# mLSTM iterations of a hybrid decoder layer: scores first, transposes of h in the second block, VectorE scales h late, ScalarE evacuates the transposes

## What is computed

```python
Dm = jnp.exp(jnp.where(causal, logD, -jnp.inf))
S = jnp.einsum('bhtd,bhsd->bhts', qc, kc) * Dm
num = jnp.einsum('bhts,bhsv->bhtv', S, vc) + g[..., None] * jnp.einsum('bhtd,bhdv->bhtv', qc, C)
den = jnp.sum(S, axis=-1) + g * jnp.einsum('bhtd,bhd->bht', qc, n)
h = num / jnp.maximum(jnp.abs(den), jnp.exp(-m_t))[..., None]
C_new = decay[..., None, None] * C + jnp.einsum('bhs,bhsd,bhsv->bhdv', w, kc, vc)
...
h = _rms(h, g_mh).astype(x.dtype).reshape(B, T, M_WIDTH)
m_out = jax.nn.sigmoid(om) * h * jax.nn.silu(zm)
```

## Time and profile before

| | |
|---|---|
| median of 3 runs | 566.33 us (566.26 to 566.77) |
| the profiled execution's own time | 566.57 us |
| its span, first to last instruction | 564.8 us |
| TensorE busy | 552.8 us (98%) |
| VectorE busy | 309.3 us (55%) |
| ScalarE busy | 225.0 us (40%) |
| GpSimd busy | 139.6 us (25%) |
| mean granted TensorE clock | 0.996 of full speed |

### The profile page before, as it was taken

The page is one execution under the profiler, slowest core; times in us unless marked ns, Lnnn a source line. Parts: engine busy times, 40 slices in busy tenths (PEclk is TensorE's granted clock), DMA queues, the critical chain, the costliest instruction groups (busy, mean ns, idle before and its releaser), DMA issues.

```text
span 564.8 us, 10012 instructions
## 1 busy us (share of the span) xinstructions
PE 552.8 (98%) x3999; PEld 511.7 (91%) x3999; DVE 309.3 (55%) x598; ACT 225.0 (40%) x591; POOL 139.6 (25%) x140
## 2 busy tenths in 40 slices
PE   7999999999999999999999999999999999999994
PEld 7999999999999999999989888899999998888773
DVE  5720002492656565521377777534676667778837
ACT  6852221423354434521355454233413126545422
POOL 1001122112334233332011211135533531001203
PEclk9999999999999999999999999999999999999998
DMA  8752210823111011007014231454121003203425
GB/s 312 294 201 76 66 38 3 252 89 85 38 39 38 3 38 39 9 32 182 9 38 141 63 79 57 114 209 165 39 75 37 1 1 111 75 1 118 161 77 204
DMA packets 31606, 50.98 MB, mean 90 GB/s; under 512 B 4460, under 2 KB 23148, under 8 KB 30904
## 3 DMA queue, kind: packets, MB, share of 16 engines
q1 hardware_dynamic: 31128, 49.82, 27.6%
q10 hardware_dynamic: 432, 0.53, 0.3%
HBM read 42.74 MB, written 8.05 MB: 90 GB/s over the span
## 4 chain that ended last, share of the span: by engine, by line
PE 92%; DVE 3%; DMA 1%; issue 1%; ACT 1%; POOL 1%; DVEq 0%; SPq 0%; ACTq 0%
PE ps L627 52%; PE ps L887 4%; PE ps L886 4%; PE ps L885 4%; PE ps L565 3%; PE ps L566 3%; PE ps L567 3%; PE ps L679 2%; PE ps L739 2%; PE ps L804 1%; PE ps L570 1%; PE ps L569 1%; PE ps L780 1%; PE ps L816 1%; PE ps L702 1%
## 5 line engine op out<-in xcount | busy, mean ns | idle before, releaser
L627 PE MATMUL ps<-x_hl,w_hi 128*128 128x364 f32 (+1 forms) x1200 | 303.0, 332 | 1.8 <-DVE x_hl L1277 1.0
L627 PEld LDWEIGHTS ps<-x_hl,w_hi 128*128 128x128 f32 x1200 | 211.1, 188 | 9.7 <-issue 6.5
L627 PE MATMUL ps<-x_hl,w_lo 128*128 128x364 f32 (+1 forms) x600 | 197.9, 330 | 0.0
L627 PEld LDWEIGHTS ps<-x_hl,w_lo 128*128 128x128 f32 x600 | 112.8, 188 | 0.1
L1847 POOL TENSOR_TENSOR qmT<-qmT,sg 128x364 f32<-128x364 f32 (+1 forms) x24 | 35.1, 1465 | 48.8 <-DVE sg L1661 29.0
L1045 ACT ACTIVATE prob<-prob,nmx 128x192 f32<-128x192 f32 (+1 forms) x64 | 27.9, 437 | 45.9 <-DVE sd L1425 45.9
L1799 POOL TENSOR_TENSOR prob<-prob,rden 128x768 f32<-128x768 f32 (+1 forms) x16 | 22.6, 1413 | 72.2 <-DVE rden L1431 72.2
L565 PE MATMUL ps<-wt_hi,x_hl 128*128 128x324 f32 x128 | 39.9, 311 | 0.0
L567 PE MATMUL ps<-wt_hi,x_hl 128*128 128x324 f32 x128 | 39.8, 311 | 0.0
L566 PE MATMUL ps<-wt_lo,x_hl 128*128 128x324 f32 x128 | 39.8, 311 | 0.0
L365 POOL TENSOR_TENSOR w_lo<-w_raw,w_hi 128x1024 fp32r<-128x1024 f32 x12 | 28.7, 2395 | 42.6 <-ACT w_hi L968 42.6
(11 more groups left out here) (286 smaller groups left out, 946.5 us busy)
## 6 DMA issues: line engine op xcount, KB each, us to landing
w_raw<-in_w_in_tiles SPq DMA_DIRECT2D x24, 512.0 KB, 3.6
x_tok<-in_x_prompt SPq DMA_DIRECT2D x8, 512.0 KB, 5.7
x_res<-in_x_prompt SPq DMA_DIRECT2D x8, 512.0 KB, 4.7
wt_raw<-in_w_tok SPq DMA_DIRECT2D x4, 648.0 KB, 8.0
logw<-lw_rows SPq DMA_DIRECT2D x8, 256.0 KB, 4.4
Cs<-in_state_C SPq DMA_DIRECT2D x16, 128.0 KB, 2.5
out_C_sample<-Cs SPq DMA_DIRECT2D x16, 128.0 KB, 1.9
wq_a<-in_w_out_blocks SPq DMA_DIRECT2D x2, 1024.0 KB, 6.6
```

Source lines behind the costliest of these rows:

```text
L627: last = mm(ps[:, sub_bank(sub), 0:w], wt, xm, start=(at_ == 0), stop=(at_ == 23))
```

## The change

It does these things, all in the mLSTM stage:

- TensorE's iteration becomes: scores of unit it, numerator and state update of unit it-1, 12 projection matmuls, transposes of h of unit it-2, `sample_inter` and `sample_round` of round it-1, transposes of k, 12 projection matmuls. `numerator(0)` of the samples moves to the start of iteration 10, the last two transposes of h to the middle of iterations 10 and 11.
- `sample_inter` writes into columns 364 on of the projection bank whose sub has just been evacuated, no more into bank 4. So it waits for that sub's evacuation and no longer for `st_done`; `sample_round` no longer waits for `it_evac`, and a sub that reuses such a bank does.
- `h_transposes` waits for `sd_mul` of the same iteration, `m_scores` for `hT_evac` of three units before.
- VectorE: mask first, then evacuation, gate of q, scores times decay, then denominator, state, mean square, low parts of weights, `inter_second`, and only then the scaling of h, which now also waits for `hT_done` of the unit before.
- ScalarE: takes over the evacuation of the transposes (four `ACT.Copy` with `gmh` as scale), writes the squares into buffers of their own (`h_junk`) instead of `hs`, and so no longer waits there for `hT_done`; `d_exp` comes first, `g_exp` one iteration early at the end.

```diff
+    h_junk = [sb(f"h_junk{h}", [P, P], F32, at_) for h, at_ in enumerate((n + 25728, n + 26240, Wr + 9216, Wr + 9728))]
...
-    IT0 = 320
+    IT0 = 364
+
+    def inter_bank(r):
+
+        return sub_bank(S_P3 + r)
...
+                    if S_P3 + 2 <= sub < S_P3 + 2 + N_ROUND:
+                        wait(pe, "it_evac", sub - S_P3 - 1)
...
         def m_scores(u):
...
-            wait(pe, "hT_evac", u - 2)
+            wait(pe, "hT_evac", u - 3)
...
         def sample_inter(r):
...
-            wait(pe, "st_done", r)
+            wait(pe, "proj_free", S_P3 + r + 1)
...
-                last = mm(ps[PQ * c:PQ * (c + 1), 4, IT0:IT0 + W1], qmT[:, h, T_P + PQ * half:T_P + PQ * (half + 1)],
+                last = mm(ps[PQ * c:PQ * (c + 1), inter_bank(r), IT0:IT0 + W1], qmT[:, h, T_P + PQ * half:T_P + PQ * (half + 1)],
...
         def sample_round(r):
             h, q = r // 2, r % 2
             wait(pe, "st_done", r)
-            wait(pe, "it_evac", r + 1)
...
         def h_transposes(u, it):
...
-            wait(pe, "sd_done", min(it, NTILE))
+            wait(pe, "sd_done", min(it + 1, NTILE))
...
         for it in range(S_P4 - S_P3):
-            if 3 <= it <= NC + 1:
-                h_transposes(it - 2, it)
-            if 2 <= it <= NC + 1:
-                numerator(it - 1)
-                state_update(it - 1)
-            project(7)
-            if it == NC + 2:
-                h_transposes(NC, it)
-                numerator(0)
             if it <= NC:
                 m_scores(it)
+            if 2 <= it <= NC + 2:
+                numerator(it - 1 if it <= NC + 1 else 0)
+            if 2 <= it <= NC + 1:
+                state_update(it - 1)
+            project(12)
+            if it >= 3:
+                h_transposes(it - 2 if it <= NC + 2 else 0, it)
             if 1 <= it <= N_ROUND:
                 sample_inter(it - 1)
-            project(7)
-            if it == NC + 3:
-                h_transposes(0, it)
-            if 1 <= it <= N_ROUND:
                 sample_round(it - 1)
             if it <= NC:
                 k_transposes(it)
-            project(10)
+            project(12)
...
         def h_squares(u):
...
             wait(act, "hden_done", v)
-            wait(act, "hT_done", v - 1)
             wait(act, "hq_ready", v - 1)
...
+        def hT_evac(u):
+            _, off, n = unit_tokens(u)
+            v = H_ORDER.index(u) + 1
+            wait(act, "hT_done", v)
+            for h in range(MH):
+                last = A_(qmT[:, h, off:off + n], ps[:, 1, h * n:(h + 1) * n], ACT.Copy, scale=gmh[:, h:h + 1])
+            last.then_inc(s("hT_evac"), 1)
+
+        g_exp(0)
         for it in range(S_P4 - S_P3):
             if it <= NC:
-                g_exp(it)
+                d_exp(it)
             if 2 <= it <= NC + 2:
                 h_squares(it - 1 if it <= NC + 1 else 0)
+            if it >= 3:
+                hT_evac(it - 2 if it <= NC + 2 else 0)
...
-            if it <= NC:
-                d_exp(it)
             if it <= NC:
                 k_weight(it)
+            if it < NC:
+                g_exp(it + 1)
             evac(S_P3 + it)
...
         for it in range(S_P4 - S_P3):
-            evac(S_P3 + it - 1)
-            if it >= 3:
-                hT_evac(it - 2 if it <= NC + 2 else 0)
-            done = None
-            if 2 <= it <= NC + 2:
-                done = it - 1 if it <= NC + 1 else 0
-                h_denominator(done)
             if it <= NC:
                 mask_weights(it)
-            if 2 <= it <= NC + 1:
-                state(it - 1)
-            if 1 <= it <= N_ROUND and it % 2 == 0:
-                inter_second(it - 1)
-            if done is not None:
-                h_mean_square(done)
-                h_scale(done)
+            evac(S_P3 + it - 1)
             if it <= NC:
                 q_gate(it)
                 sd_mul(it)
             if it == 0:
                 sample_extras()
+            done = None
+            if 2 <= it <= NC + 2:
+                done = it - 1 if it <= NC + 1 else 0
+                h_denominator(done)
+            if 2 <= it <= NC + 1:
+                state(it - 1)
+            if done is not None:
+                h_mean_square(done)
             if it >= 1:
                 splits(S_P3 + it - 1)
+            if 1 <= it <= N_ROUND and it % 2 == 0:
+                inter_second(it - 1)
+            if done is not None:
+                h_scale(done)
```

More of the change, by code:

```diff
@@ L1122, in h_squares @@
             wait(act, "hden_done", v)
-            wait(act, "hT_done", v - 1)
             wait(act, "hq_ready", v - 1)
             for h in range(MH):
-                last = A_(hs[0:n, h, :], ps[0:n, 2 + h // 2, (h % 2) * W1:(h % 2) * W1 + MD], ACT.Square,
+                last = A_(h_junk[h][0:n, :], ps[0:n, 2 + h // 2, (h % 2) * W1:(h % 2) * W1 + MD], ACT.Square,
                           accum_out=hss[0:n, h:h + 1])
             last.then_inc(s("sq_done"), 1)
+        def hT_evac(u):
[6 more added lines that the diff above has]
+        g_exp(0)
         for it in range(S_P4 - S_P3):
             if it <= NC:
-                g_exp(it)
+                d_exp(it)
             if 2 <= it <= NC + 2:
                 h_squares(it - 1 if it <= NC + 1 else 0)
+            if it >= 3:
+                hT_evac(it - 2 if it <= NC + 2 else 0)
             if 1 <= it <= N_ROUND and it % 2 == 1:
                 wait(act, "it_done", it)
-                A_(ITs[:, it // 2, :], ps[:, 4, IT0:IT0 + W1], ACT.Copy, scale=inter_msk[:, 0:1]).then_inc(s("it_evac"), 1)
-            if it <= NC:
-                d_exp(it)
+                A_(ITs[:, it // 2, :], ps[:, inter_bank(it - 1), IT0:IT0 + W1], ACT.Copy, scale=inter_msk[:, 0:1]).then_inc(s("it_evac"), 1)
             if it <= NC:
                 k_weight(it)
+            if it < NC:
+                g_exp(it + 1)
             evac(S_P3 + it)
@@ L1522, in inter_second @@
             part = ITs[:, r // 2, :]
-            STT(out=part, in0=ps[:, 4, IT0:IT0 + W1], scalar=inter_msk[:, 1:2], in1=part, op0=ALU.mult, op1=ALU.add)\
+            STT(out=part, in0=ps[:, inter_bank(r), IT0:IT0 + W1], scalar=inter_msk[:, 1:2], in1=part, op0=ALU.mult, op1=ALU.add)\
                 .then_inc(s("it_evac"), 1)
@@ L1551, in h_scale @@
             wait(dve, "hf_ready", v)
+            wait(dve, "hT_done", v - 1)
             TT(hs[0:n, :, :].rearrange("p (b h) v -> p b h v", b=2), num_view(n)[:, :, :, 0:MD],
@@ L1554, in h_scale @@
                 .then_inc(s("h_done"), 1)
[L1556 to L1561, removed]
         def splits(sub):
```

## The result

The changed kernel takes **562.94 us** (median of 4 runs, 562.81 to 563.21) against 566.51 us of the kernel before on the same chip (566.26 to 566.77, 4 runs): a ratio of 0.9935, with a 95% interval of 0.9923 to 0.9947, or 3.57 us less. The forecast was 563.8, the range 562.6 to 565.6.

A forecast was written before the change was run, and what follows sets the result against it. TensorE, busy for 98% of the span, was taken to bound the kernel. Terms of -2.6, -0.9, +0.9 and +0.15 sum to -2.5 us, from 566.33 to 563.8 us, range 562.6 to 565.6.

The forecast's parts named there:

- The stall goes: TensorE at the transposes of h: scores times decay comes earlier on VectorE, transposes later; 2.61 us of stalls go.
- The new wait and what is queued behind it: VectorE: `sd_mul` waits for the numerator, denominator and state follow; 1.85 us left at the transposes, 0.9 at `sample_round`.
- The rival of a new wait at `sample_round`: TensorE loses 0.25 us in two of three iterations, 1.3 us come back; chance 0.12, shared with dear edges.
- Scaling of h: Last on VectorE, after 1.76 us of waiting for GpSimd; 2.2 us left before the next numerator needs it.
- Evacuation on ScalarE: Four evacuations of the transposes of h take 1.14 us on ScalarE, hidden with 2.2 us to spare.
- Edges: TensorE's changes of tile shape: one of three goes per iteration at 0.10 us each, -0.9 us over eight.
- lower end (-2.5, both free): Case for TensorE's shape changes in which both new ones cost nothing: -2.5 us instead of -0.9.
- the sentence of the Trainium skill: Weight loads overlap only into other row groups; fewer shape changes on TensorE would then save nothing, sum 564.7 us.
- The start: Iteration 0 opens with the samples' scores, which wait for the last q sub's evacuation: +0.9 us, once.
- The end of the stage: Iterations 9 to 11: two more transposes of h have a projection matmul behind them, +0.15 us; samples' numerator 0.
- The rival that the gain is lost before the end: After the mLSTM stage, weights loaded after C is stored come too late: 566 us; chance 0.03.
- The distance from scores to scores: Sign on TensorE that the forecast is right: 9.6 to 9.7 us in every one of iterations 3 to 8.

The follow-up runs named there:

- experiment 3: Kernel before, with only VectorE's scaling of h moved behind the gate of q and scores times decay: 563.63 us, ratio 0.9955.
- experiment 4: Changed kernel with VectorE's gate of q and scores times decay moved behind denominator and state: 566.95 us, ratio 1.0013 to the kernel before.
- experiment 5: Changed kernel with evacuation of the transposes of h back on VectorE: 562.76 us, against 562.52 for the changed kernel in the same set.
- experiment 2: Changed kernel with seven of the last 12 projection matmuls put between `sample_inter` and `sample_round`: 564.02 us, ratio 0.9962 to the kernel before.
- Experiment 1: Changed kernel with the samples' scores of iteration 0 behind the first 12 projection matmuls: 561.79 us, ratio 0.9921 to the kernel before.
- experiment 6: Kernel before with VectorE's gate and scores times decay ahead of scaling h, `sample_inter` directly ahead of `sample_round` and in projection banks: 561.81 us, ratio 0.9925.

## Why the prediction was right, and where its sizes were off

The mechanism and the sign were right, and the time lies inside the range of 562.6 to 565.6, near its lower end. Of the forecast 2.5 us less, 3.6 came. By the parts of the prediction:

1. *The stall goes*, -2.61: right. No idle is booked at L856, and experiment 3 got 2.41 by VectorE's order alone, without the hole that belongs to `sample_inter`. The working took an iteration of 9.79 us as clean, where 9.77 is the average (experiment 3), so the stalls were rather 2.7. Scores times decay starts at N+0.30 (306.98 against 306.68) rather than N+0.20; 1.75 us are left, worked out 1.85.
2. *The new wait and what is queued behind it*: right. State ends at 308.38 + 1.12 = 309.50 = N+2.82, worked out N+2.73, and `sample_round` comes at 310.45 = N+3.77, as worked out. 0.8 us are left, worked out 0.9. The rival of a new wait at `sample_round` didn't come true. A wait of such a size did in experiment 4, at the transposes, where denominator and state are ahead of scores times decay: 4.46 us are lost.
3. *Scaling of h*, end at N+5.5: 321.79 with N = 316.25 is N+5.54. In iterations 4 and 7 it was N+6.45 (313.13 in iteration 4) because of GpSimd's slow operation. The prediction put the low parts of weights into the wait for GpSimd and took that for free. It was not free, but the margin covered it: the numerator came at N+7.78 (314.46), so 1.2 us were left of the 2.2.
4. *Evacuation on ScalarE*, hidden: right in size (1.14 us for four) and in margin (2.1 us), and experiment 5 shows that it brings nothing either.
5. *Edges*, -0.9: **the step that was mis-sized**. "I take 0.10 for each, as at the two nearest edges, which are entries into the same two shapes": transposes to `sample_inter` did cost 0.09, but `sample_inter` to `sample_round` cost nothing. That makes -1.76 by the two periods and -1.62 by experiment 2. The prediction priced an edge by the shape that is entered, where the shape that is left counts too. This term alone is 0.7 to 0.9 of the 1.1 us between forecast and result. Its lower end (-2.5, both free) held. By the sentence of the Trainium skill that was weighed there ("TensorE: Matmul & The Clock Gate", section "Part 3: Packing small matmuls — row/col tiling"), loads of full-height tiles would stand exposed and fewer edges would save nothing. Experiment 2 speaks against using it so: with the fewer edges undone, 1.62 us came back.
6. *The start*, +0.9: the hole is 0.78, net 0.69. VectorE evacuated at once when the sub was done (274.05 against 274.11), and 0.09 of the delay was an edge paid before as well. Experiment 1 took back 0.76, some 0.07 of it from an edge.
7. *The end of the stage*, +0.15: about nothing, and no wait of the samples' numerator. The prediction had the 0.07 from a single projection matmul behind transposes. With two high-part matmuls following, the three together take what they took:

```profile
356.58 0.60 PE L856 MATMUL ps<-ident,hs 128*128 128x128 f32 x4
356.93 0.58 PE L634 MATMUL ps<-x_hl,w_hi 128*128 128x364 f32 x2
357.35 0.33 PE L634 MATMUL ps<-x_hl,w_lo 128*128 128x364 f32 x1
```

   From the transposes to the low-part matmul it is 0.77, which is 0.43 + 2 x 0.166 and 0.01 over.

The rival that the gain is lost before the end is out: the middle ends behind the 100 us of later projections, and there the 3.68 us are whole. The distance from scores to scores, predicted as 9.6 to 9.7, was 9.56 to 9.59, just under it, by the same mis-sized edge.

What stays open is why one edge is free. Both tiles are narrow, one in columns (128 x 32) and one in rows (32 x 128), and the runs don't tell which of the two makes it so, since no run puts `sample_round` ahead of `sample_inter`. Nor do they tell whether the edge would be free if both wrote into the same bank, as they did before: in every run that has the two side by side, `sample_inter` writes into a projection bank and `sample_round` into banks 4 and 5.

## What to carry to other kernels

When TensorE stalls on a product of another engine, look first at what stands ahead of the producer in that engine's own order. Moving one call gave 2.4 of the change's 3.7 us here, without touching TensorE's order, and a version that keeps the old order on TensorE, but for the place of `sample_inter`, beat the full rearrangement by 0.7 us (experiment 6 against the change in the same set, 561.81 and 562.52). Try small matmuls of unlike shape next to each other, not between large ones: what was paid here is the ways in and out, some 0.1 us each, and for the one pair that was tried (128 x 32 and 32 x 128) nothing between. That other pairs are as cheap isn't shown. And when work is reordered, look at the first round by itself, since the matmuls that used to cover a producer there may be gone.

## What the runs showed of the hardware that was not expected

- A change of tile costs by both sides. Into 128 x 32 tiles 0.09 to 0.10 us and into 32-row tiles from projections 0.10, out of the 128 x 32 ones to projections 0.11, out of the 32-row ones to projections at least 0.11 and to transposes at least 0.06, from the 128 x 32 into the 32-row ones 0.00, and between two kinds of full-size transposes 0.00. ("At least", because `sample_round` alone was never measured without such a step behind it.)
- A tiny operation of GpSimd (128 x 4) took 1.14 us instead of 0.23 while VectorE ran one of 1.22 us over 128 x 1024 elements, ended nearly with it (311.01 and 310.92), and was back at 0.23 once the two were apart. Where GpSimd's small operations lie on a path that matters, the long operation of VectorE beside them is part of their price.
